# Rotating halves of 32 rows by VectorE's shuffle instead of TensorE's products

## The reference

```python
def _rope(x, cos, sin):                      # first block, 32 channels of q and k in "mla"
    x1, x2 = jnp.split(x, 2, axis=-1)
    return jnp.concatenate([x1 * cos - x2 * sin, x1 * sin + x2 * cos], axis=-1)

def _rope_2(x, pos):                         # second block
    d = x.shape[-1]
    ...
    x1, x2 = x32[..., :half], x32[..., half:]
    return jnp.concatenate([x1 * cos - x2 * sin, x2 * cos + x1 * sin], axis=-1).astype(x.dtype)

def _axial_rope(x, row, col):                # branch A: two halves of 32 channels each
    half = x.shape[-1] // 2
    return jnp.concatenate([_rope_2(x[..., :half], row), _rope_2(x[..., half:], col)], axis=-1)
```

## Time and profile before

| what | value |
|---|---|
| time, median of 3 runs | 1445.62 us (1444.1 to 1446.26) |
| time of the profiled execution | 1441.98 us |
| its span in the profile | 1440.2 us |
| TensorE (PE) busy | 1370.3 us, 95% of the span |
| VectorE (DVE) busy | 871.3 us, 60% |
| ScalarE (ACT) busy | 732.9 us, 51% |
| GpSimd (POOL) busy | 382.7 us, 27% |

### The profile page before, as it was taken

One profiled execution on the slowest core, in us unless ns is written; L12 is line 12 of the kernel. 1 busy time (PEld: TensorE's weight loads), 2 busy tenths in 40 slices (PEclk: granted clock), 3 DMA queues, 4 the chain that ended last, 5 costly groups with the idle time before them and its releaser, 6 DMA issues.

```text
span 1440.2 us, 20040 instructions
## 1 busy us (share of the span) xinstructions
PE 1370.3 (95%) x7454; PEld 1064.4 (74%) x7454; DVE 871.3 (60%) x1519; ACT 732.9 (51%) x1561; POOL 382.7 (27%) x273
## 2 busy tenths in 40 slices
PE   7999999999989999999998899999899999999897
PEld 7876788778787677887776877676766877675665
DVE  4656536557663674455577675468656665578555
ACT  4555447655244554556554464446444554546443
POOL 2233131346131322213554111321012111421111
PEclk9999999999999999999999999999999999999999
DMA  7413551126252221112265432511324343511311
GB/s 237 118 31 92 115 143 48 50 72 226 102 161 59 58 91 59 59 49 66 77 237 164 125 77 56 125 59 52 103 67 91 111 91 71 112 59 23 118 52 59
DMA packets 185894, 135.65 MB, mean 94 GB/s; under 512 B 91334, under 2 KB 166726, under 8 KB 185798
## 3 DMA queue, kind: packets, MB, share of 16 engines
q1 hardware_dynamic: 182022, 120.22, 30.9%
q10 hardware_dynamic: 3776, 14.16, 2.5%
HBM read 122.03 MB, written 12.32 MB: 93 GB/s over the span
## 4 chain that ended last, share of the span: by engine, by line
PE 70%; DVE 15%; ACT 8%; issue 2%; POOL 2%; DMA 1%; SPq 1%; DVEq 0%; ACTq 0%; POOLq 0%
PE pb L1652 18%; PE pb L1654 17%; PE pb L1653 17%; PE pb L1743 5%; PE pb L1692 5%; PE pb L1719 5%; ACT prob L1798 3%; ACT tmp L1798 2%; DVE wl L2168 2%; DVE prob L2428 2%; SPq L2706 1%; ACT wh L1818 1%; PE pb L1773 1%; POOL wl L2572 1%; DMA tbias<-zscr 1%
## 5 line engine op out<-in xcount | busy, mean ns | idle before, releaser
L2572 POOL TENSOR_TENSOR wl<-wr,wh 128x512 fp32r<-128x512 f32 x178 | 252.7, 1420 | 708.9 <-ACT wh L1818 704.8
L1652 PE MATMUL pb<-xh,wl 128*128 128x512 f32 (+1 forms) x880 | 351.0, 399 | 11.8 <-DVE wl L2168 6.4
L1654 PE MATMUL pb<-xh,wh 128*128 128x512 f32 (+1 forms) x880 | 325.8, 370 | 0.0
L1653 PE MATMUL pb<-xl,wh 128*128 128x512 f32 (+1 forms) x880 | 325.5, 370 | 0.0
L2168 DVE TENSOR_TENSOR wl<-wr,wh 128x512 fp32r<-128x512 f32 x208 | 169.6, 818 | 166.1 <-ACT wh L1818 165.7
L1818 ACT CAST wh<-wr 128x512 fp32r<-128x512 f32 (+1 forms) x386 | 220.3, 606 | 35.9 <-PE pb L1654 16.8
L1652 PEld LDWEIGHTS pb<-xh,wl 128*128 128x128 f32 x880 | 168.4, 191 | 65.4 <-issue 29.5
L1654 PEld LDWEIGHTS pb<-xh,wh 128*128 128x128 f32 x880 | 168.3, 191 | 29.0
L1653 PEld LDWEIGHTS pb<-xl,wh 128*128 128x128 f32 x880 | 169.0, 192 | 24.7 <-issue 4.3
L1652 PE MATMUL pb<-wh,xl 128*128 128x256 f32 (+1 forms) x320 | 109.1, 341 | 10.1 <-DVE wl L2168 7.9
L2052 ACT COPY prob<-pb 128x512 f32<-128x512 f32 (+3 forms) x128 | 61.4, 480 | 110.3 <-PE pb L1719 109.9
(11 more groups left out here) (199 smaller groups left out, 2340.3 us busy)
## 6 DMA issues: line engine op xcount, KB each, us to landing
wr<-w_in SPq DMA_DIRECT2D x39, 1024.0 KB, 5.3
wr<-w_out SPq DMA_DIRECT2D x14, 1024.0 KB, 5.1
wr<-w_in SPq DMA_DIRECT2D x48, 256.0 KB, 4.5
wr<-w_branch SPq DMA_DIRECT2D x48, 128.0 KB, 2.3
x<-prob SPq DMA_DIRECT2D x12, 512.0 KB, 3.6
wr<-w_mem_kv SPq DMA_DIRECT2D x4, 1024.0 KB, 5.7
prob<-x ACTq DMA_DIRECT2D x2, 2048.0 KB, 11.0
wr<-w_out SPq DMA_DIRECT2D x16, 256.0 KB, 4.4
```

The lines of the kernel that those rows point to most:

```text
L1652: e.matmul(ps, ll, rh, start=start, stop=False)
L1653: e.matmul(ps, lh, rl, start=False, stop=False)
L1654: t = e.matmul(ps, lh, rh, start=False, stop=stop)
L2572: t = e.tensor_tensor(wl[:, j % 2, c0:c1], wr[:, j % 2, c0:c1], wh[:, j % 2, c0:c1].bitcast(F32), ALU.subtract)
```

## The change

Rotations within 32 rows (mla's, A's and D's) are no longer products. VectorE's instruction `stream_shuffle`, with a list of 32 places that is used in each group of 32 rows, copies the source into the temporary with its halves swapped; the sign stands in the sine table (for A and D in the table in memory, for mla by a column of -1 and +1 with which ScalarE scales the angle before it takes the sine). VectorE then multiplies the temporary in place. B's rotations, across 64 rows, stay as they are. The steps take no PSUM bank, and the planner counts nothing for them.

```diff
+    put("sign", np.where(p % 32 < 16, -1.0, 1.0))
...
-            rows_s.append(np.sin(ang))
+            rows_s.append(-np.sin(ang) if d == 32 and r % 32 < 16 else np.sin(ang))
...
-    if k in ("dqk", "squares", "rope1", "rope2", "qsquares", "dsquares"):
+    if k in ("dqk", "squares", "qsquares", "dsquares") or k == "rope2" and s["br"] == "B":
         return 860
...
         def turn_rope(part, src):
-            b, t2 = GR[0].take(), TM.take()
-            put("rope1", l=l, part=part, src=src, b=b, tm=t2)
-            give(b, t2)
+            t2 = TM.take()
+            put("rope1", l=l, part=part, src=src, tm=t2)
+            give(t2)
...
-        b, t2 = GR[0].take(), None if br == "A" else TM.take()
+        b, t2 = GR[0].take() if br == "B" else None, None if br == "A" else TM.take()
...
+    HALVES = [(j + 16) % 32 for j in range(32)]
...
-            elif k == "rope1":
-                b = s["b"]
...
-                t = e.matmul(bank(b), C("rot16"), src, start=True, stop=True)
-                t.then_inc(aux.sem, aux.mark(b))
-            elif k == "rope2":
+            elif k == "rope2" and s["br"] == "B":
...
-                act(sin1, ang, ACT.Sin).then_inc(a_fn.sem, a_fn.mark())
+                act(sin1, ang, ACT.Sin, C("sign")).then_inc(a_fn.sem, a_fn.mark())
...
             elif k == "rope1":
...
-                w.wait_ge(aux, aux.at(b))
...
-                e.tensor_tensor(t2, bank(b), sin1, ALU.mult).then_inc(v_fn.sem, v_fn.mark(ends=(b,)))
+                w.wait_ge(v_copy, v_copy.at(("krope", l) if part == "k" else ("qb", s["src"])))
+                e.stream_shuffle(t2, src, HALVES).then_inc(v_fn.sem, v_fn.mark())
+                w.wait_ge(v_fn, v_fn.n)
+                e.tensor_tensor(t2, t2, sin1, ALU.mult).then_inc(v_fn.sem, v_fn.mark())
                 e.tensor_tensor(src, src, cos1, ALU.mult).then_inc(v_fn.sem, v_fn.mark())
...
-                e.tensor_tensor(t2, bank(b), tabs[:, 1, :], ALU.mult).then_inc(v_fn.sem, v_fn.mark(ends=(b,)))
+                if br == "B":
+                    w.wait_ge(aux, aux.at(b))
+                    e.tensor_tensor(t2, bank(b), tabs[:, 1, :], ALU.mult).then_inc(v_fn.sem, v_fn.mark(ends=(b,)))
+                else:
+                    w.wait_ge(a_copy, a_copy.at(("pair", s["src"])))
+                    e.stream_shuffle(t2, src, HALVES).then_inc(v_fn.sem, v_fn.mark())
+                    w.wait_ge(v_fn, v_fn.n)
+                    e.tensor_tensor(t2, t2, tabs[:, 1, :], ALU.mult).then_inc(v_fn.sem, v_fn.mark())
```

More of the change, by code:

```diff
@@ L71, in constants @@
     put("bones", (p // 64) == (c // 64))
[L72 to L80, removed]
+    m = np.zeros((P, P))
+    for j in range(P):
+        if j % 64 < 32:
+            m[j + 32, j] = -1
+        else:
+            m[j - 32, j] = 1
+    put("rot32", m)
     put("causal", np.concatenate([np.zeros((P, 384)), np.where(c > p, NEG, 0.0)], 1))
@@ L147 @@
     tensor_tensor_reduce = tensor_reduce = tensor_tensor_scan = reciprocal = memset = op
-    bn_stats = bn_aggr = dma_start = op
+    bn_stats = bn_aggr = dma_start = stream_shuffle = op
 class Waits:
@@ L1179, in behind @@
             yield
-        b, t2 = GR[0].take(), None if br == "A" else TM.take()
+        b, t2 = GR[0].take() if br == "B" else None, None if br == "A" else TM.take()
         put("rope2", l=l, br=br, n=n, src=tm, b=b, tm=t2)
-        give(b, *[t2] * (br != "A"))
+        give(*[b] * (br == "B"), *[t2] * (br != "A"))
         if br == "A":
@@ L1444, in build @@
     biases = [setB[:, 3072:3968], setA[:, 4096:4992], tbias[:, 0, :], tbias[:, 1, :]]
-    ROT = {"A": ("rot16", 0), "B": ("rot32", 2), "D": ("rot16", 4)}
+    TABLE = {"A": 0, "B": 2, "D": 4}
+    HALVES = [(j + 16) % 32 for j in range(32)]
     SCALE = {"mla": float(96 ** -0.5)}
@@ L1772, in tensor_program @@
                 w.wait_ge(a_copy, a_copy.at(("pair", s["src"])))
-                t = e.matmul(bank(b), C(ROT[s["br"]][0]), tm(s["src"]), start=True, stop=True)
+                t = e.matmul(bank(b), C("rot32"), tm(s["src"]), start=True, stop=True)
                 t.then_inc(aux.sem, aux.mark(b))
@@ L2284, in vector_program @@
             elif k == "rope1":
-                l, part, b, t2 = s["l"], s["part"], s["b"], tm(s["tm"])
+                l, part, t2 = s["l"], s["part"], tm(s["tm"])
                 src = kp if part == "k" else tm(s["src"])
-                w.wait_ge(aux, aux.at(b))
                 for g, v in s["tm"].free():
@@ L2692, in sync_program @@
                 for q in range(2):
-                    t = e.dma_start(tabs[:, q, :], a["tables"][ROT[br][1] + q])
+                    t = e.dma_start(tabs[:, q, :], a["tables"][TABLE[br] + q])
                     t.then_inc(d_tab.sem, d_tab.mark((l, br)))
```

## The result

The changed kernel takes 1449.84 us (median of 11 runs, 1447.17 to 1453.1), beside 1442.02 us of the kernel before (11 runs, 1441.09 to 1446.81). The ratio is 1.0047 with an interval of 1.0035 to 1.0059: slower by about 6.8 us (5.0 to 8.5), where the forecast was 0.2% faster and the range ended at 1448.0. The profiled execution took 1450.41 us, its span is 1448.6 (before 1440.2).

The account below looks back on a forecast made before the run. TensorE is busy 95% of the span, but VectorE bounds mla's stretch; per layer +1.20 - 0.06 - 2.58 = -1.44, for two layers -2.9 us, giving 1442.7 us (0.2% faster), range 1437.0 to 1448.0.

Parts of the forecast that it names:

- The prices: A rotation's product takes 0.86 us of TensorE; a shuffle takes 0.69 us and adds 0.72 us to VectorE.
- The base: Profiled execution of the kernel before, 1441.98 us, with the median of the runs taken as 3.6 us above it.
- the two fast ends: Faster shuffles on the mla and A chains, -2.2 us in all; one GpSimd stall fewer on each of four chains, 3.9.
- A's rotations: Six products; TensorE's 2.58 us saving before A's first logits becomes -0.06 us a layer, as VectorE's tile comes 0.74 later.
- The stalls beside GpSimd: VectorE instructions on A's chain taking 1.67 us instead of 0.69 beside GpSimd's chunks; as many assumed as before.
- D's rotations: Six products beside B's attention; VectorE's 3.85 us of slack covers the shuffles, so -2.58 us a layer is real.
- a rival: D's gain lost: shuffles delay VectorE's copies of turned probabilities that TensorE awaits; gives back up to 5.2 us; chance 0.15.
- mla's rotations: Four products; VectorE's chain to the gate's weight chunk grows, so TensorE's wait ends later: +1.20 us a layer.
- What else moves: Product pieces and casts change places in the memory attention and B's attention; counted as nothing, 1 us either side.
- The last rival: The new order opens a gap in the memory attention or B's: within 2 us of no change; chance 0.08.
- only makes its wait longer: At mla's rotations, TensorE's saving of 1.72 us a layer only lengthens its wait for VectorE's weight chunk.
- The lock: Multiplications now reading two SBUF tiles stall beside GpSimd; one more stall for each of ten adds 9.8 us; chance 0.14.

Follow-up runs that it names:

- old order: Planner still counts 860 ns per shuffled rotation, so nothing else moves; against the kernel before: mla's shuffles only 1.0029, D's only 0.9992, all three 1.0013.

## Why the prediction was wrong

**The prices** held: a shuffle takes 0.74 for 0.69, and the 0.86 us for a product were not tested by themselves. The base did not: the 3.6 us between the profiled execution and the median came from three runs, and the median of eleven is 1442.02. From there the forecast of 0.2% means 1439.1, so it missed by more than 1442.7 beside 1449.84 says. The lower end of the range, 1437.0, does not follow from the two fast ends given (half of 2.2 and 3.9 leads to 1439.6); it played no part.

**A's rotations** (-0.06 a layer): right. A gained 0.25 at its logits, with a wait of 1.89 where 2.5 was expected, and alone gives 1.0005. The stalls beside GpSimd, taken as many as before, came to 4.1 us before and 3.9 after on this chain of the first layer.

**D's rotations** (-2.58 a layer): right in size, wrong in reason. Both layers show 2.5 to 2.6, D alone 0.9958. But "this gain is real" was argued from VectorE's rotated tiles, and the copies between them were left to a rival. In the old order only 0.7 us a layer arrive, since the shuffles and the stalls behind them delay B's copy and reciprocals; the other 1.9 come from the planner's new order. The rival had set the planner's spacing against this, without a size, so that the gain came out at its full size was in part luck.

**mla's rotations** (+1.20 a layer): the mechanism was right, and the chain by itself costs 0.76 in the old order. In the changed kernel it is 1.67, as the last of VectorE's weight chunks now runs beside GpSimd's (0.95 of it).

**"What else moves ... so I count nothing, with 1 us to either side"**: this step failed. TensorE's rotations also stood in the planner's clock: with two of them counted at nothing, the projections that fill mla's stage count less in all, the attention's steps are spaced more closely (this is read from the planner's program, not tested by itself), and in the memory attention TensorE asks for turned probabilities (1.23) and exponentials (1.18) that aren't there yet. The last rival named such a gap, with a chance of 0.08, but held it to within 2 us of no change. "There TensorE waits on chains that start from its own work" was true, but such a chain has a length, and the matmuls between cover it or don't. The order costs 2.8 us a layer up to the wait's end; in mla's part alone it makes 1.0078 of 1.0029. In B's attention the same edit has the other sign.

**TensorE's clock** was in no step. The prediction wrote that the saving "only makes its wait longer". A longer wait was not free here: behind 3.2 to 3.8 us of it the granted clock was 0.50, and 1.4 to 2.4 us were lost each time in the profiles of the changed kernel and of mla alone in the old order; with work in the wait, nothing. This is the term that was missing from the sum, 3.8 us for both layers at mla alone, and some of A's waits (0.56 from 1175.6 on) pay it too.

**The lock** as the rival had it, one more stall for each of the new multiplications, is out: A and D alone would have shown it. VectorE is busy for 17.9 us more, 11.8 of them in the sixteen shuffles, so all its stalls together grew by some 6 us, and in A's and D's parts without a loss. Its place in the result is the 0.95 us a layer of the chunk at 133.71, 1.9 of the 6.8, which the order brought about.

So my sum of -2.9 us becomes +5.3: D -5.1, A -0.5, mla's chain in the old order +1.5, the new order in mla's stage +5.6, the clock behind the two long waits +3.8. Measured are 6.8; the rest is within the ratio's interval (from 5.0).

## What to carry to other kernels

Taking work from TensorE in front of a wait lengthens the wait, and a longer wait can halve the clock of what follows, as it did here; price the wait's end and then the matmuls behind it, and where the other engine can't be made faster, give TensorE idle products or leave its work where it was. An edit that changes a planner's costs is two edits: separate them by keeping the old cost once, since the moved order can cost more than the edit, or pay for it. Of a change with several places, do each alone: here the part worth having (D, 0.9958) was hidden by one that wasn't (mla, 1.0078).

## What the runs showed of the hardware

A shuffle of 128x512 float32 takes 0.72 to 0.75 us in the changed kernel, and its mask's load does not delay it (6 to 15 ns, at the same start). TensorE's granted clock fell to 0.50 behind waits of 3.18 to 3.76 us behind mla's rotations, in both layers of all four profiles that have them, and not behind 1.62 at the same place; filled with products of zeros down to 0.59 and 0.31 us of idle time, the same places stay at 1.00. Elsewhere, waits of 1.7 to 1.9 us had a half clock within 3 us behind them in some profiles and not in others (42 of 129 in the fourteen profiles), those of 2.4 us always (26 of 26).

The scatter between runs of one kernel goes with the clock. Of the 84 runs of the kernel before beside the experiments, the eleven with a mean granted clock of 0.990 or more took 1440.2 to 1442.3 us, the thirteen with 0.985 or less 1444.2 to 1447.6. So a single profile's end says little about a difference of 3 us.
